# Three steps of gate and up at a feed-forward's opening, closings by half rows, wide products in a row, in a two-block kernel

## The reference, cut to what matters

```python
def swiglu(x, w_gate, w_up, w_down):
    return (jax.nn.silu(x @ w_gate) * (x @ w_up)) @ w_down
...
    for layer in range(DEPTH_2):
        if layer == N_A_LAYERS:
            k, v, c = shared_kv(h, kv_norm_g, w_kv, w_fgate, b_fgate)
        f = swiglu(rms_norm_2(h, ffn1_pre_g[layer]), ...)
        h = h + 0.5 * rms_norm_2(f, ffn1_post_g[layer])
        hn = rms_norm_2(h, mix_pre_g[layer])
        ...                       # m: recurrent_block or forgetting_attention
        h = h + rms_norm_2(m, mix_post_g[layer])
        f = swiglu(rms_norm_2(h, ffn2_pre_g[layer]), ...)
        h = h + 0.5 * rms_norm_2(f, ffn2_post_g[layer])
```

## Time and profile before

| | |
|---|---|
| Median of 3 runs | 1554.76 us (1553.53 to 1554.89) |
| Profiled execution, its own time | 1554.81 us |
| Its span, first to last instruction | 1553.0 us |
| Mean granted TensorE clock | 0.997 |
| TensorE matmuls busy | 1503.0 us (97%) |
| VectorE busy | 1203.0 us (77%) |
| ScalarE busy | 789.9 us (51%) |
| 16 DMA engines | 54.1% on the weights' queue |

### The profile page before, as it was taken

How to read it: one execution, slowest core, us unless ns; L and a number is a source line. 1 busy time by engine, 2 the same in 40 slices (tenths; PEclk the granted TensorE clock), 3 DMA queues, 4 the chain that set the end, 5 groups by cost and what they waited for, 6 DMA issues and landing times.

```text
span 1553.0 us, 23704 instructions
## 1 busy us (share of the span) xinstructions
PE 1503.0 (97%) x8186; PEld 1281.3 (83%) x8186; DVE 1203.0 (77%) x2164; ACT 789.9 (51%) x1193; POOL 43.5 (3%) x68
## 2 busy tenths in 40 slices
PE   7989999999999899999999999999999999999997
PEld 6767789888888788887878888888888889888886
DVE  4876477988888888778588878785888886597876
ACT  6547554444434544446796444465544466554443
POOL 4100000000000300000000000000000000000000
PEclk9999999999999999999999999999999999999999
DMA  9635445755555666655244766644766643366661
GB/s 257 186 92 185 136 136 209 264 192 181 193 187 160 172 209 196 189 174 175 66 123 139 227 179 198 189 138 152 209 197 189 189 139 107 106 184 191 195 187 57
DMA packets 258538, 266.16 MB, mean 171 GB/s; under 512 B 10512, under 2 KB 210496, under 8 KB 258224
## 3 DMA queue, kind: packets, MB, share of 16 engines
q1 hardware_dynamic: 255040, 255.87, 54.1%
q0 software_dynamic: 3440, 9.54, 2.1%
HBM read 264.21 MB, written 1.09 MB: 171 GB/s over the span
## 4 chain that ended last, share of the span: by engine, by line
PE 85%; DVE 10%; ACT 3%; issue 2%; DMA 0%; DVEq 0%; SPq 0%; ACTq 0%
PE ps L733 25%; PE ps L649 13%; PE ps L650 13%; PE ps L651 13%; PE ps L735 11%; DVE w_lo L1955 2%; PE ps L732 2%; PE ps L1209 1%; DVE xT_both L1999 1%; PE ps L1352 1%; PE ps L675 1%; ACT w_hi L1455 1%; DVE xn L2164 1%; PE ps L659 0%; ACT xT_both L1464 0%
## 5 line engine op out<-in xcount | busy, mean ns | idle before, releaser
L733 PE MATMUL ps<-xT_both,w_hi 128*128 128x512 f32 x1392 | 492.3, 398 | 1.3 <-DVE w_lo L1960 1.3
L1518 ACT ACTIVATE w_hi<-raw 128x1024 fp32r<-128x1024 f32 x294 | 308.3, 1057 | 159.1 <-PE ps L651 137.0
L1960 DVE TENSOR_TENSOR w_lo<-raw,w_hi 128x1024 fp32r<-128x1024 f32 x294 | 350.5, 1220 | 1.6 <-ACT w_hi L1518 0.2
L735 PE MATMUL ps<-xT_both,w_lo 128*128 128x256 f32 x1218 | 342.1, 281 | 0.0
L733 PEld LDWEIGHTS ps<-xT_both,w_hi 128*128 128x128 f32 x1392 | 256.1, 188 | 52.0 <-DVE w_lo L1960 1.8
L1955 DVE TENSOR_TENSOR w_lo<-raw,w_hi 128x1024 fp32r<-128x1024 f32 (+4 forms) x191 | 225.6, 1211 | 37.7 <-ACT w_hi L1455 35.8
L735 PEld LDWEIGHTS ps<-xT_both,w_lo 128*128 128x128 f32 x1218 | 230.3, 189 | 6.7
L1513 ACT ACTIVATE hid_sil<-hid_sil 128x256 f32<-128x256 f32 x120 | 50.1, 418 | 360.6 <-DVE hid_sil L2025 320.7
L1455 ACT ACTIVATE w_hi<-raw 128x1024 fp32r<-128x1024 f32 (+4 forms) x191 | 193.0, 1048 | 29.6 <-PE ps L651 25.8
L649 PE MATMUL ps<-w_hi,hid_hi 128*128 128x512 f32 x480 | 188.8, 393 | 4.2 <-DVE hid_lo L2072 4.1
L650 PE MATMUL ps<-w_lo,hid_hi 128*128 128x512 f32 x480 | 187.1, 390 | 0.0
(11 more groups left out here) (393 smaller groups left out, 2181.5 us busy)
## 6 DMA issues: line engine op xcount, KB each, us to landing
raw<-in_ffn_w_gate_dram SPq DMA_DIRECT2D x88, 512.0 KB, 4.2
raw<-in_ffn_w_up_dram SPq DMA_DIRECT2D x88, 512.0 KB, 5.3
raw<-in_ffn_w_down_dram SPq DMA_DIRECT2D x88, 512.0 KB, 4.2
raw<-in_w_in_dram SPq DMA_DIRECT2D x40, 512.0 KB, 4.9
raw<-in_w_gate_dram SPq DMA_DIRECT2D x32, 512.0 KB, 3.5
raw<-in_w_up_dram SPq DMA_DIRECT2D x32, 512.0 KB, 4.1
raw<-in_w_down_dram SPq DMA_DIRECT2D x32, 512.0 KB, 3.5
raw<-in_rg_w_in_dram SPq DMA_DIRECT2D x16, 512.0 KB, 4.6
```

What stands on the lines that cost most here:

```text
L733: m = pe.matmul(o, hi[:, k, :], both[:, :, k, :], start=k == 0, stop=k == KT - 1)
L735: pe.matmul(ps[:, bank, 0:T], lo[:, k, :], both[:, 0, k, :], start=False, stop=False)
L1518: act.activation(w_hi[:, s, :], raw[:, s, :], ACT.Copy).then_inc(hi_done, 1)
L1960: dve.tensor_tensor(w_lo[:, s, :], raw[:, s, :], w_hi[:, s, :].bitcast(F32), ALU.subtract)\
```

## The change

1. In `channel_major_wide` seven 512-column products come first, then all eight 256-column ones, then the eighth 512-column one. The same sixteen matmuls.
2. ffn0, ffn1 and ffn3 open with steps 1 and 2 ahead of the first down product: first pair, `spread`, gate and up of step 1, gate and up of step 2, down of steps 0 and 1, gate and up of step 3, down of step 2, and the loop from step 4. The pieces change their order in the ring on all engines (`LEAD` replaces `AHEAD`). ACT loads silu's table before it copies `rb`. `moe` and `ffn2` keep their order.
3. The softplus chain moves from ffn0 to the recurrent stage, between the remainders of piece 14 and `input_gate(0)`.
4. Closings go by half rows: a new semaphore `y_half` tells that half row 0 of a tile is complete. Tile 1's products are ordered half 0 first, then half 1 (in feed-forwards 6 and 6 matmuls, in `rgout` and `out` 9 and 9, in `o` 6 and 6 behind piece 5). ACT squares a half when it is complete, DVE's gain product of a half waits for its square, and `residual` adds by half rows; so `norm_group` and `statistics` of norms 1 and 2 wait for both halves. In `out` the transposes of tile 0 stand between the halves of tile 1.

```diff
-        AHEAD = {"moe": 3, "ffn0": 1, "ffn1": 1, "ffn2": 0, "ffn3": 1}
         SPREAD = {"ffn0": 2, "ffn1": 4, "ffn3": 8}
+
+        LEAD = {"moe": 4, "ffn0": 3, "ffn1": 3, "ffn2": 1, "ffn3": 3}
...
+                elif LEAD[ph] == 3:
+
+                    for f in range(4):
+                        at = b + (0, 3, 5, 9)[f]
+                        if f == 3:
+                            piece(b + 7, flat, row_piece(ph, wd, 0))
+                            piece(b + 8, flat, row_piece(ph, wd, 1))
+                        piece(at, square, col_piece(ph, wg, f))
+                        piece(at + 1, square, col_piece(ph, wu, f))
+                    piece(b + 11, flat, row_piece(ph, wd, 2))
                 else:
                     step(0)
                     step(1)
 
-                with sp.Fori(2 if ph == "moe" else 1, n // 2) as g:
+                with sp.Fori(2 if LEAD[ph] > 1 else 1, n // 2) as g:
...
-                elif g == 0 and (n < 3 or t and n != 6):
-                    pe.wait_ge(x_part, X_PART[n] + t * (n < 3))
+                elif n < 3:
+
+                    pe.wait_ge(x_part, X_PART[n] + t)
+                    pe.wait_ge(x_ready, X_AT[n] - 1 + t)
+                elif g == 0 and t and n != 6:
+                    pe.wait_ge(x_part, X_PART[n])
                 else:
                     pe.wait_ge(x_ready, X_AT[n] - 1 + t)
...
+                for k in range(KT - 1):
+                    pe.matmul(o, hi[:, k, :], both[:, :, k, :], start=k == 0, stop=False)
                 for k in range(KT):
-                    if k == KT - 1:
-                        pe.matmul(ps[:, bank, 0:T], lo[:, k, :], both[:, 0, k, :], start=False, stop=False)
-                    m = pe.matmul(o, hi[:, k, :], both[:, :, k, :], start=k == 0, stop=k == KT - 1)
-                    if k < KT - 1:
-                        pe.matmul(ps[:, bank, 0:T], lo[:, k, :], both[:, 0, k, :], start=False, stop=False)
+                    pe.matmul(ps[:, bank, 0:T], lo[:, k, :], both[:, 0, k, :], start=False, stop=False)
+                m = pe.matmul(o, hi[:, KT - 1, :], both[:, :, KT - 1, :], start=False, stop=True)
...
+                def down_part(s, par, t, h, first, last):
+
+                    c = slice(t * P, (t + 1) * P)
+                    r = slice(h * WID, (h + 1) * WID)
+                    return mm3(ps[:, 2 * t + h, :], hid_hi[:, par, c], hid_lo[:, par, c],
+                               w_hi[:, s, r], w_lo[:, s, r], first, last)
+
...
+                    between()
+                    one_up(b + 3, 5)
+                    one_up(b + 4, 7)
+                    one_up(b + 5, 4)
+                    one_up(b + 6, 6)
+                    down(c0 + 1, b + 7, 0, True, False, s=(b + 7) % RING)
+                    down(c0 + 2, b + 8, 1, False, False, s=(b + 8) % RING)
+                    one_up(b + 9, 5)
+                    one_up(b + 10, 7)
+                    down(c0 + 3, b + 11, 0, False, False, s=(b + 11) % RING)
                 else:
-                    if norm_n is None:
-                        up_narrow(b, 0, PLAN.step(b + 1))
-                    else:
-                        first_pair(norm_n, b, (ps[:, 0, 0:T], ps[:, 1, 0:T]), (1, PLAN.step(b + 1)))
+                    up_narrow(b, 0, PLAN.step(b + 1))
                     up(1, b + 3, 1, between)
-                    if after_second:
-                        after_second()
+                    after_second()
                     down(c0 + 1, b + 5, 0, True, False)
-                with pe.Fori(4 if ph == "moe" else 2, n - 2, 2) as f:
+                with pe.Fori(4 if LEAD[ph] > 1 else 2, n - 2, 2) as f:
                     for par in range(2):
...
-                down(c0 + n - 1, b + 3 * n - 1, 0, False, False, tiles=(0,))
-                down(c0 + n, b + 3 * n, 1, False, True, s=s, tiles=(0,))
-                down(c0 + n - 1, b + 3 * n - 1, 0, False, False, tiles=(1,))
-                down(c0 + n, b + 3 * n, 1, False, True, s=s, tiles=(1,))
+                s0, s1 = (b + 3 * n - 1) % RING, (b + 3 * n) % RING
+                pe.wait_ge(hid_ready, c0 + n - 1)
+                pe.wait_ge(lo_done, b + 3 * n)
+                for h in range(2):
+                    down_part(s0, 0, 0, h, False, False)
+                pe.wait_ge(hid_ready, c0 + n)
+                pe.wait_ge(lo_done, b + 3 * n + 1)
+                down_part(s1, 1, 0, 0, False, True).then_inc(y_half, 1)
+                down_part(s1, 1, 0, 1, False, True).then_inc(y0_done, 1)
+                down_part(s0, 0, 1, 0, False, False)
+                down_part(s1, 1, 1, 0, False, True).then_inc(y_half, 1)
+                down_part(s0, 0, 1, 1, False, False).then_inc(used, 1)
+                down_part(s1, 1, 1, 1, False, True).then_inc(used, 1)
 
             pe.wait_ge(sig("ident_in"), 16)
 
...
+                for j in range(RN):
+                    for h in range(2):
+                        m = rg_part(g, j, 0, h)
+                        if j == RN - 1:
+                            m.then_inc((y_half, y0_done)[h], 1)
+                for h in range(2):
+                    for j in range(RN):
+                        m = rg_part(g, j, 1, h)
+                        if h:
+                            m.then_inc(used, 1)
+                        elif j == RN - 1:
+                            m.then_inc(y_half, 1)
 
             def rg_in(first, last):
...
-                    r = slice(h * WID, (h + 1) * WID)
-                    m = mm3(ps[:, 2 * t + h, :], oT_hi[:, k, c], oT_lo[:, k, c], w_hi[:, s, r], w_lo[:, s, r],
-                            k == 0, k == KT - 1)
-                if t:
-                    m.then_inc(used, 1)
-                elif k == KT - 1:
-                    m.then_inc(y0_done, 1)
+                    o_part(k, t, h)
...
                 b, c0 = PLAN.start[ph], HID0[ph]
-                for f in (0, 1) if ph != "moe" else ():
-
-                    for i in (b + 3 * f + 3, b + 3 * f + 4, b + 3 * f + 5)[0 if f else AHEAD[ph]:]:
+                if LEAD[ph] == 3:
+
+                    hi(b + 4)
+                    hi(b + 5)
+                    act.activation(s_(S_WARM), C("eps"), ACT.Silu)
+                    spread(SPREAD[ph], 3)
+                    silu(c0 + 1, 0)
+                    hi(b + 6)
+                    hi(b + 7)
+                    silu(c0 + 2, 1)
+                    for i in range(b + 8, b + 11):
                         hi(i)
-                    if f == 0 and ph in SPREAD:
-                        spread(SPREAD[ph], 3)
-                    silu(c0 + f + 1, f)
-
-                with act.Fori(4 if ph == "moe" else 2, n - 2, 2) as f:
+                    silu(c0 + 3, 0)
+                    for i in range(b + 11, b + 13):
...
                 for t in range(NT):
-                    if t == 0:
-                        act.wait_ge(y0_done, half)
-                    else:
-                        act.wait_ge(used, w)
                     for h in range(2):
-                        if h and t == 0:
-                            act.wait_ge(y_gained, 4 * j + 1)
+                        if h == 0:
+                            act.wait_ge(y_half, 4 + 2 * j + t + 1)
+                        elif t == 0:
+                            act.wait_ge(y0_done, half)
+                        else:
+                            act.wait_ge(used, w)
                         act.activation(sq[:, t, h * WID:(h + 1) * WID], ps[:, 2 * t + h, :], ACT.Square,
                                        accum_out=s_(S_YSQ + 2 * t + h)).then_inc(y_ssq, 1)
-                    act.wait_ge(y_ssq, 4 * j + 2 * t + 2)
-                    link(act.activation(s_(S_YB + t), s_(S_YSQ + 2 * t + 1), ACT.Identity, bias=C("eps"), scale=1.0 / D))
-                    act.activation(s_(S_YSQRT + t), s_(S_YSQ + 2 * t), ACT.Sqrt, bias=s_(S_YB + t), scale=1.0 / D)\
+                        act.wait_ge(y_ssq, 4 * j + 2 * t + h + 1)
+                        if h == 0:
+                            link(act.activation(s_(S_YB + t), s_(S_YSQ + 2 * t), ACT.Identity, bias=C("eps"), scale=1.0 / D))
+                    act.activation(s_(S_YSQRT + t), s_(S_YSQ + 2 * t + 1), ACT.Sqrt, bias=s_(S_YB + t), scale=1.0 / D)\
                         .then_inc(y_sqrt, 1)
 
...
                     dve.wait_ge(sig("comb_in"), 32)
+                elif LEAD[ph] == 3:
+                    lo(b + 4)
+                    lo(b + 5)
+                    dve.wait_ge(norm_rb, RB_AT[norm_n])
+                    scale_gate(b + 1, 0, 0)
+                    lo(b + 6)
+                    hidden(c0 + 1, b + 3, 0, None, c0 + 1, None, 1)
+                    scale_gate(b + 4, 1, 5, w0 + 1)
+                    lo(b + 7)
+                    hidden(c0 + 2, b + 5, 1, None, c0 + 2, None, 7, both=w0 + 1)
+                    lo(b + 8)
+                    scale_gate(b + 6, 0, 4, w0 + 2)
+                    lo(b + 9)
+                    lo(b + 10)
```

(48 more changed lines are left out.)

138 lines of the change are left out of this document (78 added, 60 removed).

## The result

The changed kernel takes 1543.94 us (median of 4, 1542.71 to 1545.22); the kernel before, timed beside it, 1554.18 (4 runs, 1553.53 to 1554.89). The ratio is 0.9933, 95% interval 0.9918 to 0.9949: about 10 us faster. The forecast was 1541.0, the range 1537.5 to 1548.0, so the sign and the range held and the gain was smaller than forecast. The profiled execution of the changed kernel took 1542.71 (span 1540.8); against the profiled one of before (1554.81, span 1553.0) that is 12.2 us of span, where I had forecast 13.8.

What follows compares the result with a forecast made beforehand. TensorE, busy 97% of the span, was taken to bound the kernel. Order 6.6, openings with softplus 4.5 and closings 2.7 sum to 13.8 us off 1554.8, giving 1541.0; range 1537.5 to 1548.0.

Steps and rivals of the forecast that it cites:

- Part 1: Matmul order within channel_major_wide calls: wide and narrow products in rows save 6.6 us; bounds nothing and 7.7.
- 0.062 off, times 107 = 6.6 us: Feed-forward gate and up pairs: each falls from 5.63 to 5.57 us, over 107 pairs.
- upper bound: Most the matmul order could save: 7.7 us, if narrow products in a row take 0.1193 each.
- Part 2: Openings of ffn0, ffn1, ffn3: the hid_lo wait, 1.3 each, goes; net 1.2 in ffn0, 0.9 in the others.
- new wait: At the early spread in ffn1 and ffn3: TensorE waits 0.4 us for diag; under 0.1 in ffn0.
- Part 3: Softplus moved from ffn0 into DVE's idle time before input_gate(0): TensorE's wait at 536.86 goes, 1.5 us.
- Part 4: Closings by half rows: 0.8 us each at rgout and o, 0.27 at four others; sum 2.7, bounds 0 and 4.5.
- Order worth nothing: Rival on matmul order in channel_major_wide: reordering saves nothing, total 1547.6 us; chance 0.10.
- Two-block operand at 0.235 throughout: Rival: every L733 wide product stays at 0.235, +5.4 us in all, total 1553.0; chance 0.05.
- DVE falling behind: Rival in the three reordered openings: another wait of 1.3 us in each, total 1544.9; chance 0.08.
- covers: Reordered openings: DVE results ready ahead of use, remainder for up of step 2 3.5 us, hid 0 4.5, smallest 1.7.
- The clock at `diag`: Rival: early spread waits 4.2 us for diag and the clock drops, three openings cost 17.7, total 1558.7; chance 0.03.

Runs made afterwards that it cites:

- Experiment 1: The kernel before with only the new matmul order inside channel_major_wide (seven wide, eight narrow, one wide): 1551.35 us, ratio 0.9979.
- 5: The changed kernel with 96 unused bytes ahead of arena: 1542.44 us, ratio 0.9922.
- 6: The changed kernel with 96 unused bytes ahead of arena and the old alternating order put back: 1548.62 us, ratio 0.9962.
- second kernel: The changed kernel with the old alternating order put back in channel_major_wide, all else of the change kept: 1547.72 us, ratio 0.9956.

## Why the prediction held, and where it was off

**Part 1, order: the direction right, the term mis-sized.** The step that failed is "0.062 off, times 107 = 6.6 us". First, behind a row of narrow products about five wide ones come late, not two. Within the pair that cost nothing against the forecast, since the narrow ones came closer by as much: all sixteen wide ones take 3.66 (3.65 forecast), the narrow ones 1.90 (1.92), and the pair 5.567 (5.568). But the delay reaches into the down products, which I had left as they were and which went from 2.727 to 2.741: 0.053 a step in place of 0.062, some 0.8 us over 87 pairs. Second, I read both prices in ffn1 and applied them to all feed-forwards. The trace had ffn2's steps, 8.30 against 8.36, and its own group of 320 records at 393 ns against 398; I quoted that row and did not ask why it differed. There the order costs 0.027 a step: the 20 pairs of its loop steps give +0.5 where I had -1.2. Together 2.5 us less, of the 2.7 that are missing: 3.9 by the traces, 3.2 by the timed medians (1.9 to 4.7), for 6.6. Experiments 1, 5 and 6 show it. A slip besides: with narrow ones at 0.1193 the upper bound comes to 7.8, not 7.7.

The rule of the Trainium skill ("TensorE: Matmul & The Clock Gate", Back-to-back issue gap) that the prediction quotes, a gap by column count alone, which the section calls that of an isolated matmul, would make the order worth nothing. Experiment 1's interval excludes that here, and the table of steps has eight values for one set of products.

**Part 2, openings: right.** From the start of the first pair's last sixteen products to the down product of step 2, ffn1 took 867.72 - 841.58 = 26.14 before and 861.71 - 836.48 = 25.23 in the second kernel, 0.9 less, as forecast (1.3 less 0.4), and ffn3 went the same way, 26.11 to 25.14; the table's 1.2 for ffn1 has kv's closing in it. The new wait is 0.23 idle, 0.39 by starts. In ffn0, with softplus gone, it is 542.66 - 514.86 = 27.80 and 538.77 - 513.78 = 24.99, 2.8 for a forecast of 1.2 + 1.5.

**Part 3, softplus: right.** 1.5 forecast; PE's wait of 1.34 idle goes, and alone it measured 1.8 (0.5 to 3.6).

**Part 4, closings: right.** No run has them alone; this goes by the waits of the traces and the stages of the table. The forecast was 0.8 for each of rgout and `o`, and 0.27 elsewhere. The recurrent stage's close gave 0.73 of PE's wait and q with `o` 0.65; kv's and q's first residual waits fell from 0.79 to 0.50 at the close of the feed-forward, the last ones stayed (0.66 and 0.65). Parts 2 to 4: 7.2 forecast, 7.6 by the trace of the second kernel, 6.8 timed (4.7 to 8.9).

**The rivals.** Order worth nothing: excluded by experiment 1, although for ffn2 it was nearly so. Two-block operand at 0.235 throughout: not in the other feed-forwards; in ffn2 products at 0.234 did appear, from the buffer's place. DVE falling behind: covers were 3.7 and 4.9 where I had 3.5 and 4.5, and the smallest 2.0 where I had 1.7. The clock at `diag`: that wait was 0.23, and from 826 to 851 us, around it, the granted clock was 1.00.

**The sum.** Order 3.9 for 6.6, the rest 7.6 for 7.2, and 0.7 by scatter before moe: 12.2 for 13.8. Against the median 1543.94 instead of the profiled 1542.71 there is a further 1.2: the profiled execution was the fastest of four, and that of before was among the slower ones of its kind (1554.8; 1553.3 to 1555.4 over 21 runs).

## What to carry to other kernels

Before a price per instruction is multiplied by a count, look whether every group of the same shape has it; a few ns between two groups of one shape, over thousands of matmuls, is a microsecond, and here it had a cause that could be found. Where TensorE is 97% busy, try where the operands lie relative to the other buffers: here 32 to 128 bytes of padding decided over 12 us, more than the whole change. And where a wait remains, ask what the waiting instruction really needs: a product that writes another bank than those being evicted can go first and cover the eviction.

## What was not expected of the hardware

The spacing of matmuls depends on where their operands' buffers lie relative to the buffers ahead of them: wide products in a row 0.227 apart where the distance from `w_hi` is 0 modulo 512 bytes, 0.231 to 0.234 at the others tried, and steps of 8.30 to 8.42 for the same 44 products. The narrow ones need not follow: 0.114 at 448, 0.119 at 0. The alternating order is shorter in ffn2's place (8.30) than in the aligned one (8.36), the order in rows the other way round (8.327 and 8.307). Nor is the spacing a matter of a product's own operands alone: the down products of ffn1 went from 2.73 to 2.74 when only the order before them changed, those of ffn2 from 2.72 to 2.76 when `arena` moved, which they don't read.

In six of the fourteen traces, none of them that of the kernel before or of the changed one, 14 to 16 narrow products at the start of ffn0's first pair took 0.213 instead of 0.120 each, 1.3 to 1.5 us in all. Timeline of PE and windows (columns as in the earlier trace rows) of the kernel with the order alone, then the windows of the changed kernel:

```profile
510.22 0.42 PE L753 MATMUL ps<-xT_both,w_hi 128*128 128x256 f32 x1
510.43 0.41 PE L754 MATMUL ps<-xT_both,w_lo 128*128 128x256 f32 x1
...
507.00:511.00 4.00, 2.34 (x16) 2.14 (x15) 3.67 (x15) 4.00 (x15) 3.80 (x1) 0.88 0.05 18
511.00:515.00 4.00, 4.00 (x27) 4.00 (x26) 3.54 (x15) 3.93 (x8) 3.71 (x6) 0.70 0.24 43
```

```profile
507.00:511.00 4.00, 2.29 (x19) 2.29 (x20) 4.00 (x16) 4.00 (x13) 3.71 (x2) 1.00 0.00 0
511.00:515.00 4.00, 4.00 (x34) 3.81 (x33) 3.44 (x14) 3.93 (x8) 4.00 (x7) 1.00 0.53 127
```

0.213 is 256 columns at 1.2 GHz, and the granted clock says the same. It comes just behind TensorE's wait of 1.7 for ACT's evictions, which all fourteen traces of these kernels have; what decides whether the clock falls in one execution and not in another was not found. By its size it could be part of the scatter of about 2 us among executions of one kernel, which is not shown, since each kernel has one trace; and it is a reason not to read a difference of 1.5 us from one profile.
